# Storing the sums of the first three token tiles one at a time, each behind its own additions

## The reference

```python
gates = (one_hot(idx, N_EXPERTS) * sel[..., None]).sum(1)      # 2 of 16 experts a token
h = silu(einsum('nd,edf->nef', xt, w_gate)) * einsum('nd,edf->nef', xt, w_up)
y = einsum('nef,efd->nd', h * gates[..., None], w_down)
shared = (silu(xt @ ws_gate) * (xt @ ws_up)) @ ws_down
x = layer_norm(DEEPNORM_ALPHA * x + (y + shared))
```

## Time and profile before

| | us |
|---|---|
| median of 3 runs | 1217.55 |
| lowest and highest | 1215.06 and 1222.80 |
| profiled execution, its time | 1218.93 |
| profiled execution, its span | 1217.1 |
| share of the span in which PE was busy | 98% |
| mean granted clock of PE, of 1 | 0.997 |

### The profile page before, as it was taken

One profiled execution on the slowest core, in us unless ns is written; L12 is line 12 of the kernel. 1 busy time (PEld: TensorE's weight loads), 2 busy tenths in 40 slices (PEclk: granted clock), 3 DMA queues, 4 the chain that ended last, 5 costly groups with the idle time before them and its releaser, 6 DMA issues.

```text
span 1217.1 us, 22117 instructions
## 1 busy us (share of the span) xinstructions
PE 1198.4 (98%) x8040; PEld 1076.1 (88%) x8040; DVE 724.5 (60%) x1796; ACT 591.5 (49%) x1463; POOL 218.2 (18%) x276
## 2 busy tenths in 40 slices
PE   9999999999999999999999999999999999999998
PEld 9998888888888888888777888899989999999896
DVE  3222455655565556555877778568856566656358
ACT  4332344544454445444552434254557666756566
POOL 1121001200120012001211211000224323423223
PEclk9999999999999999999999999999999999999999
DMA  9787674365436643667854333592999999999995
GB/s 277 225 300 226 156 195 101 79 162 139 101 80 152 149 101 79 157 162 215 264 172 186 124 122 131 187 360 94 321 303 247 291 277 270 286 290 268 353 313 200
DMA packets 164676, 246.93 MB, mean 203 GB/s; under 512 B 41536, under 2 KB 111424, under 8 KB 163776
## 3 DMA queue, kind: packets, MB, share of 16 engines
q1 hardware_dynamic: 149408, 190.72, 51.4%
q0 software_dynamic: 11776, 41.95, 14.0%
q10 hardware_dynamic: 3408, 13.16, 2.7%
HBM read 150.59 MB, written 65.31 MB: 177 GB/s over the span
## 4 chain that ended last, share of the span: by engine, by line
PE 74%; issue 12%; DMA 4%; DVE 3%; POOL 3%; SPq 2%; ACT 1%; POOLq 1%; ACTq 0%; DVEq 0%
PE bank L916 16%; PE bank L918 16%; PE bank L917 16%; PE bank L1049 9%; PE bank L1036 5%; PE bank L1027 4%; PE bank L910 3%; PE bank L1028 3%; DMA raw_gu<-in_w_up 2%; POOL c_work L2509 1%; DVE c_work L2056 1%; DVE c_work L2054 1%; DVE w_gu_lo L2163 1%; SPq L615 1%; POOL Q L2536 1%
## 5 line engine op out<-in xcount | busy, mean ns | idle before, releaser
L1516 ACT ACTIVATE b_work<-b_work 128x256 f32<-128x256 f32 (+3 forms) x288 | 148.1, 514 | 230.0 <-DVE b_work L1969 230.0
L916 PE MATMUL bank<-xgT_hi,w_gu_hi 128*128 128x224 f32 (+1 forms) x704 | 195.6, 278 | 1.2 <-DVE c_work L2038 0.9
L918 PE MATMUL bank<-xgT_hi,w_gu_lo 128*128 128x224 f32 (+1 forms) x704 | 194.7, 277 | 0.0
L917 PE MATMUL bank<-xgT_lo,w_gu_hi 128*128 128x224 f32 (+1 forms) x704 | 194.7, 277 | 0.0
L1978 DVE COPY b_work<-bank 128x256 f32<-128x256 f32 (+2 forms) x256 | 112.8, 441 | 114.8 <-PE bank L1036 113.9
L916 PEld LDWEIGHTS bank<-xgT_hi,w_gu_hi 128*128 128x128 f32 x704 | 135.0, 192 | 3.0 <-issue 1.5
L917 PEld LDWEIGHTS bank<-xgT_lo,w_gu_hi 128*128 128x128 f32 x704 | 135.0, 192 | 0.8
L918 PEld LDWEIGHTS bank<-xgT_hi,w_gu_lo 128*128 128x128 f32 x704 | 135.0, 192 | 0.0
L2536 POOL CAST Q<-Q 128x512 fp32r<-128x512 f32 x48 | 53.3, 1141 | 432.1 <-DVE w_k_lo L1908 226.2
L1036 PE MATMUL bank<-keep,b_work 128*128 128x128 f32 x608 | 114.2, 274 | 3.2 <-ACT b_work L1516 3.2
L1036 PEld LDWEIGHTS bank<-keep,b_work 128*128 128x128 f32 x608 | 79.1, 139 | 36.3 <-ACT b_work L1516 8.0
(11 more groups left out here) (244 smaller groups left out, 2831.0 us busy)
## 6 DMA issues: line engine op xcount, KB each, us to landing
raw_gu<-in_w_gate SPq DMA_DIRECT2D x32, 512.0 KB, 8.7
raw_gu<-in_w_up SPq DMA_DIRECT2D x32, 512.0 KB, 9.6
raw_d<-in_w_down SPq DMA_DIRECT2D x16, 1024.0 KB, 9.7
Q<-stage_hi SPq DMA_DIRECT2D x96, 128.0 KB, 2.4
Q<-stage_lo SPq DMA_DIRECT2D x96, 128.0 KB, 2.4
o_scratch<-b_work SPq DMA_DIRECT2D x36, 264.0 KB, 3.4
wo_scratch<-a_work POOLq DMA_DIRECT2D x16, 512.0 KB, 4.4
w_o<-wo_scratch SPq DMA_DIRECT2D x16, 512.0 KB, 5.8
```

The lines of the kernel that those rows point to most:

```text
L916: nc.tensor.matmul(o, w_hi, x_hi, start=first, stop=False)
L917: nc.tensor.matmul(o, w_hi, x_lo, start=False, stop=False)
L918: return nc.tensor.matmul(o, w_lo, x_hi, start=False, stop=last)
L1516: nc.scalar.activation(prob[:, u % 2, 0:n], prob[:, u % 2, 0:n], ACT.Exp, scale=-1.0, bias=o[:, HD:HD + 1], accum_out=o[:, HD + 1:HD + 2])\
```

## The change

The function that stored all three tiles becomes one that stores one tile, and its three calls are put at three places in ACT's list: tile 0 behind the split of step 3's weights (at the end of step 2), tile 1 behind both `xg_high` of step 3, tile 2 in step 3 behind the split of step 4's weights and ahead of `xg_high(4,0)`. The waits of each tile and the DMA stay as they were, and so does the number of stores.

```diff
-            def store_early():
-
-                for tile in range(EARLY):
-                    for half in range(2):
-                        act.wait_ge(S["y_read0" if half == 0 else "y_read1"], tile + 1)
-                    act.dma_start(acc_two[tile], base[:, 2 * tile:2 * tile + 2, :]).then_inc(S["acc_st"], 16)
+            def store_early(tile):
+
+                for half in range(2):
+                    act.wait_ge(S["y_read0" if half == 0 else "y_read1"], tile + 1)
+                act.dma_start(acc_two[tile], base[:, 2 * tile:2 * tile + 2, :]).then_inc(S["acc_st"], 16)
...
                 if EARLY < n + 1 <= LATE0:
                     gu_split(q + 1, 1 - s, n + 1)
+                if n == EARLY:
+                    store_early(2)
...
-                if n == EARLY:
-                    store_early()
...
                 if n == EARLY - 1:
                     gu_split(q + 1, 1 - s, n + 1)
+                    store_early(0)
                     xg_high(q + 1, 0, n + 1)
                     xg_high(q + 1, 1, n + 1, bank[0:2])
+                    store_early(1)
```

## The result

| | before | after |
|---|---|---|
| median of 8 runs, us | 1217.70 | 1227.06 |
| lowest and highest, us | 1215.06 and 1224.03 | 1224.45 and 1229.65 |
| profiled execution, its time, us | 1218.93 | 1229.62 |
| its span, us | 1217.1 | 1227.8 |

The ratio of after to before is 1.0074, with a 95% interval of 1.0058 to 1.0091: 9.0 us, between 7.1 and 11.1. That is within the 1% that was forecast, and it is slower as forecast, but the range ended at 1224.4 and the forecast of +2.6 us was a third of what came.

What follows compares the result with a forecast made beforehand. PE, busy 98% of the span, was taken to bound the kernel. + 5.6 (load and issue) + 1.6 (half clock) - 3.0 - 1.6 (old stall) = + 2.6 us on the median 1217.55: 1220.2 us, range 1214.5 to 1224.4.

Steps and rivals of the forecast that it cites:

- What bounds the kernel, and that the stage is carried to the end unchanged: PE is busy 98% of the span; any change to its time between 850 and 897 us reaches the end unchanged.
- No wait at the moved stores, and old place without gain: Each tile's additions end before its store's new issue, so no wait; leaving the old place gives back nothing.
- Tile 2's issue costs 0.4 us on the way: On ACT ahead of `xg_high(4,0)`, the store's issue delays PE by 0.4 us (bounds 0.25 and 0.5).
- The delay of the load: Two stores, 2.10 MB, delay the load of step 4's second half by 5.2 us (bounds 0 and 6.1).
- The price of half clock behind the new wait: After PE's longer wait at `dxt`'s second half for step 4, the clock falls to 0.50, costing 1.6 us.
- rival D: More than one wait: stores at the slow rate, longer half clock, the gather's 0.7 us; +5.2 us, 1222.8, chance 0.1.
- The gather's wait: Tile 0's store may delay the second gather of step 3's rows: taken as 0, bounds 0 and 0.7 us.
- The gain from the old stall: PE's wait for `gated(4)`, 3.0 us, and the half clock behind it, 1.6 us, go: 4.6 us won.
- A: Stores are cheap at their new places and only the gain is left: -4.2 us, 1213.4, chance 0.2.
- B: Losses and gains cancel, only tile 0's store delaying the load, by 2.6 us: net 0, 1217.6, chance 0.2.
- C: The stall moves and grows, the load 5.2 us late: +2.6 us, 1220.2, chance 0.5 (net +1 to +5 us).
- the turns of the rings: Engines go round between rings a packet at a time, so the stores' delay would be somewhat under 5.2 us.

Runs made afterwards that it cites:

- e5_step4: Against the kernel before, all three stores are issued one step later, in step 4 behind the split of step 5's weights; ratio 1.0001 (0.9985 to 1.0017).
- e3_tile2: Against the kernel before, only tile 2's store is at its new place, tiles 0 and 1 at the old one; ratio 0.9999 (0.9983 to 1.0015).
- e4_no_stores: Against the kernel before, the three stores are left out and one copy of x1's rows is issued earlier instead; ratio 1.0000 (0.9981 to 1.0019).
- e2_tile1: Against the kernel before, only tile 1's store is at its new place, tiles 0 and 2 at the old one; ratio 1.0027 (1.0008 to 1.0046).
- e1_tile0: Against the kernel before, only tile 0's store is at its new place, tiles 1 and 2 at the old one; ratio 1.0034 (1.0017 to 1.0050).

## Why the prediction was wrong

**What bounds the kernel, and that the stage is carried to the end unchanged:** right. From 898 to 1175 the differences stay within 0.1 us in most profiles, and within 0.5 in all. In the last 40 us up to 1.7 us more come in, in some executions of before as well; in the first profiles of before and after it is nothing.

**No wait at the moved stores, and old place without gain:** right. Also right: in both profiles of after POOL's first adding store did not wait for the tiles' stores (it did in e5_step4 alone, for 0.8 us).

**Tile 2's issue costs 0.4 us on the way:** wrong, it costs nothing that shows. It is issued while ACT's last pieces are still at work (879.06 after), and in e3_tile2 PE has no wait there at all.

**The delay of the load:** the step that failed first. Its mechanism was right: the load took 15.50 us, PE waited, the clock fell to 0.50. Its size was 8.7 us and not 5.2. The estimate for the two stores was good: with the gather held back the load grows by 5.55 us. What it left out is what the load meets by being late. The forecast added bytes to a fixed crowd, and took its upper bound of 6.1 us from the slow rate of the same bytes; the gather of step 5's rows, at 866.86 in the profile before, stood 0.1 us ahead of the load's landing at 866.98, and a delay of 5 us was bound to run into it. That row had been there to be read. It is worth 3.2 us of load.

**The price of half clock behind the new wait:** forecast 1.6 us, measured 0.7 + 1.9 = 2.6. The clock falls during the wait and stays down for some 6 us of work behind it. The forecast named this size (2.6 us) in rival D, as a tail.

**The gather's wait:** forecast 0, measured 0.4, inside its bounds of 0 to 0.7. In the second profile of after it was 1.4 us, outside them. Tile 0's store is issued ahead of the last gathers and not behind them.

**The gain from the old stall:** the step that failed second. 4.6 us were counted; in the profiles it is 3.9, since the sum left out the 0.8 us behind the stall that PE loses once the stall is gone, and in the times the stall is worth between nothing and 2.3 us (e4_no_stores). It was read from a single execution. The trace showed a load that landed so late that PE waited 3.0 us, and a margin that thin against a transfer in a crowd is not a constant: 3.0, 0, 2.8 and 1.9 us.

**The sum again, by the profile's stage:** +8.3 for the wait (forecast 5.6), +2.6 for the clock (1.6), +0.4 for the gather (0), -3.9 for the old stall (-4.6): +7.4 us (+2.6). The timed difference is 9.0 (7.1 to 11.1), and with the average stage of the four profiles of before, 1.0 us better than the first, the profiles give 8.4.

**The rivals.** A (a gain of 4 us) and B (cancelling) are out; both rest on the credit for the old stall and on a small delay. C, the forecast itself, had the right mechanism with too small a delay and too large a credit. D, at +5.2 us with a chance of 0.1, had the nearest terms and was still too low, since its longest delay was 6.1 us. The forecast had drawn one more thing from the Trainium skill's page "DMA: Bandwidth & Descriptors", section on queues, rings and completion order: that the turns of the rings keep the delay somewhat under 5.2 us. It did not come out so: with the gather held back the load grew by 5.55 us, no less than the 5.2 us of all the stores' bytes. The runs do not contradict the turns themselves, but no saving by them shows in what the load waits.

No kernel here beats the one before. Leaving the three stores out gives 1.0000 (0.9981 to 1.0019), so no better place for them can gain more than 2.3 us.

## What to carry to other kernels

Before moving a transfer ahead of a load that the critical engine depends on, list what else is issued between that load's present landing and its delayed one: the delay is not the moved bytes over the rate, but also those of whatever the late load now meets. A credit for a stall of 0 to 3 us behind a DMA in a crowd must be read from several executions, not one, and so must what the engine would wait for next once the stall is gone. And that a store's data is ready is no reason to issue it: here three stores cost at most 2.3 us at the old place, and 9 us more with two of them ahead of a load that PE already waited 0.6 us for.

## What the runs showed that was not expected

- ACT's DMA issue doesn't wait for the activations ahead of it in ACT's list: tile 0's is at 855.13 with six of eight pieces of the split still to start. It waits only where a semaphore does: tile 2's is at 879.06, 0.06 us behind the start of the first piece that had waited for the load.
- One store of 1.05 MB ahead of the load costs it 2.7 us, one issued with it 1.7 us, both 8.7 us (5.55 us with the gather held back).
- The granted clock fell to 0.50 behind waits of 1.9, 2.8, 3.0, 5.3, 5.8, 8.1, 8.2 and 8.9 us. Behind e2_tile1's wait of 2.3 us it stayed at 1.00, and behind e1_tile0's of 2.4 us it fell, costing 1.6 us: two waits of nearly one length, two outcomes (in e1_tile0 PE had also waited 0.9 us for gathered rows, some 15 us earlier).
- The 850 us ahead of the changed stage differ by 4.1 us between four executions of one kernel.
